# Sums of squares of eight heads: two rounded passes on TensorE in place of one exact one

## The reference, cut to what matters

```python
def group_rmsnorm(o, g):
    B, L, H, dv = o.shape
    of = o.astype(jnp.float32)
    y = of * lax.rsqrt(jnp.mean(of * of, axis=-1, keepdims=True) + EPS)
    y = y.reshape(B, L, H * dv) * g.astype(jnp.float32)
    return y.astype(o.dtype)
```

## Time and profile before

| | |
|---|---|
| median of three runs | 833.07 us |
| the profiled execution's own time | 832.05 us |
| its span | 830.1 us |
| PE busy | 818.5 us, 99% |
| DVE busy | 590.2 us, 71% |
| ACT busy | 374.9 us, 45% |
| POOL busy | 215.6 us, 26% |
| mean granted TensorE clock | 0.992 of full speed |

### The profile page before, as it was taken

One profiled execution on the slowest core, in us unless ns is written; L12 is line 12 of the kernel. 1 busy time (PEld: TensorE's weight loads), 2 busy tenths in 40 slices (PEclk: granted clock), 3 DMA queues, 4 the chain that ended last, 5 costly groups with the idle time before them and its releaser, 6 DMA issues.

```text
span 830.1 us, 15746 instructions
## 1 busy us (share of the span) xinstructions
PE 818.5 (99%) x6544; PEld 807.9 (97%) x6544; DVE 590.2 (71%) x765; ACT 374.9 (45%) x524; POOL 215.6 (26%) x258
## 2 busy tenths in 40 slices
PE   9999999999999999999999999999999999999996
PEld 9999999999999999999999999999999999999996
DVE  5464668477898886767558877777777756878973
ACT  6553234232354553534343644444434424544574
POOL 4018236434335600000430333333223222000020
PEclk9999999999999999999999999999999999999998
DMA  9669967983324984537898497477687863765622
GB/s 273 212 204 164 270 218 164 194 227 134 108 103 93 209 261 140 162 105 263 178 269 229 98 262 223 140 191 186 250 213 203 228 164 96 202 182 168 179 64 107
DMA packets 163025, 152.27 MB, mean 183 GB/s; under 512 B 6677, under 2 KB 144617, under 8 KB 162940
## 3 DMA queue, kind: packets, MB, share of 16 engines
q1 hardware_dynamic: 129420, 109.73, 42.2%
q0 software_dynamic: 33376, 41.04, 26.5%
q10 hardware_dynamic: 160, 0.53, 0.2%
HBM read 145.31 MB, written 58.40 MB: 245 GB/s over the span
## 4 chain that ended last, share of the span: by engine, by line
PE 93%; DVE 4%; issue 1%; DMA 1%; ACT 0%; SPq 0%; DVEq 0%; ACTq 0%
PE mm L2034 51%; PE ax L2327 14%; PE mm L2441 8%; PE ax L2441 6%; PE ax L2053 6%; PE mm L2327 4%; PE ax L2058 2%; PE mm L2114 1%; DVE grs L1453 1%; DMA x_nat<-in_x_prompt 1%; DVE wlo L1443 1%; PE mm L2046 0%; DVE s0g L1623 0%; DVE ylo L1701 0%; DVE wlo L1713 0%
## 5 line engine op out<-in xcount | busy, mean ns | idle before, releaser
L2034 PE MATMUL mm<-nhi,whi 128*128 128x272 f32 x928 | 196.8, 293 | 0.6 <-ACT gqk L1019 0.6
L2034 PE MATMUL mm<-nhi,wlo 128*128 128x272 f32 x928 | 193.4, 290 | 0.0
L2034 PE MATMUL mm<-nlo,whi 128*128 128x272 f32 x928 | 192.7, 289 | 0.0
L1019 ACT ACTIVATE whi<-raw 128x1024 fp32r<-128x1024 f32 (+3 forms) x112 | 128.5, 1181 | 68.8 <-PE mm L2034 38.4
L2034 PEld LDWEIGHTS mm<-nhi,whi 128*128 128x128 f32 x928 | 147.6, 190 | 2.8 <-issue 1.2
L2034 PEld LDWEIGHTS mm<-nlo,whi 128*128 128x128 f32 x928 | 146.9, 190 | 0.0
L2034 PEld LDWEIGHTS mm<-nhi,wlo 128*128 128x128 f32 x928 | 146.4, 191 | 0.0
L1713 DVE TENSOR_TENSOR wlo<-raw,whi 128x1024 fp32r<-128x1024 f32 (+1 forms) x78 | 84.4, 1123 | 5.7 <-ACT whi L1019 3.2
L1443 DVE TENSOR_TENSOR wlo<-raw,whi 128x2048 fp32r<-128x2048 f32 x27 | 64.8, 2398 | 17.5 <-ACT whi L1019 17.4
L950 POOL DMA_DIRECT2D v_sums<-in_w_up x24 | 30.8, 4224 | 117.4 <-DVE mlo L1784 116.8
L1019 ACT ACTIVATE whi<-ring 128x1408 fp32r<-128x1408 f32 x25 | 34.6, 1384 | 44.1 <-PE ax L2441 24.0
(11 more groups left out here) (390 smaller groups left out, 1982.5 us busy)
## 6 DMA issues: line engine op xcount, KB each, us to landing
raw<-in_w_in SPq DMA_DIRECT2D x36, 512.0 KB, 4.9
raw<-in_w_up SPq DMA_DIRECT2D x36, 512.0 KB, 6.9
ring<-w_sums SPq DMA_DIRECT2D x16, 704.0 KB, 4.9
w_sums<-in_w_down SPq DMA_DIRECT2D x9, 768.0 KB, 10.3
w_sums<-in_w_down POOLq DMA_DIRECT2D x9, 768.0 KB, 9.9
ring<-in_w_down SPq DMA_DIRECT2D x9, 704.0 KB, 4.3
v_sums<-in_w_up SPq DMA_DIRECT2D x24, 256.0 KB, 7.1
v_sums<-in_w_up POOLq DMA_DIRECT2D x24, 256.0 KB, 14.4
```

Of the source, the lines that this page charges most:

```text
L1019: return act.activation(out, in_, func, **kw).then_inc(done, 1)
L2034: ins = pe.matmul(mm[:, 2 * j + a, 0:HALF], w, x[:, kx, HALF * a:HALF * (a + 1)], start=first and n == 0 and m == 0, stop=last and n == le ...
```

## The change

The sum of squares over partitions is split as the large products are. ACT squares the head's output twice: once into an fp32r tile (`gsq_high`, a rounded high part), once in float32 into `gsq`. DVE subtracts the high part, in place, which gives `gsq_low`, and counts up a new semaphore `osq_low`. PE waits for that one, and adds four products of 272 columns in fp32r (high and low of each half) instead of two in fp32. A copy of the ones in fp32r type is written once, before the first norm, over the same bytes. The high part has three places: for n below 7 it is one of two by n % 2, of which the even one is the buffer `grs`; so the wait for `o_ready` now stands ahead of the square of norm n and no longer ahead of its root.

```diff
+    gsq_low = at("gsq_low", [P, NT], o_rope, F32R)
+    high_at = [at(f"gsq_high{i}", [P, NT], off, F32R) for i, off in enumerate((o_rope + T, g - T, C + 11 * T))]
+    gsq_high = [high_at[n % 2 if n < 7 else 2] for n in range(2 * HEADS)]
...
+                if n == 0:
+                    st.did(act.activation(ones_r[:, :], ones, ACT.Copy))
+                if n > 1:
+                    act.wait_ge(o_ready, n - 1)
+                st.did(act.activation(gsq_high[n][:, :], normed(NORMS[n]), ACT.Square))
                 run(gsq[:, :], normed(NORMS[n]), ACT.Square, osq_done)
             elif k in ("gn", "rn"):
                 aux_wait_filled(act, s)
-                if norms > 1:
-                    act.wait_ge(o_ready, norms - 1)
                 run(halves(grs2[norms % 2][:, :]), bank2(s), ACT.Sqrt, drained_sem(s), scale=1.0 / DV, bias=eps)
...
+            elif k in ("gsq", "rsq"):
+                n = NORMS.index(("gn" if k == "gsq" else "rn", s[1]))
+                dve.wait_ge(osq_done, n + 1)
+                dve.tensor_tensor(gsq_low[:, :], gsq[:, :], gsq_high[n][:, :].bitcast(F32), ALU.subtract).then_inc(osq_low, 1)
...
+        def summed_parts(name, high, low):
+
+            aux_take(pe, name)
+            for a in range(2):
+                t = HALVES[a]
+                small(bank(name, a)[:, 0:HALF], ones_r[:, :], high[:, t], stop=False)
+                small(bank(name, a)[:, 0:HALF], ones_r[:, :], low[:, t], start=False, done=filled_sem(name) if a else None)
...
             elif k in ("gn", "rn"):
-                pe.wait_ge(osq_done, NORMS.index(s) + 1)
-                summed(s, gsq)
+                pe.wait_ge(osq_low, NORMS.index(s) + 1)
+                summed_parts(s, gsq_high[NORMS.index(s)], gsq_low)
```

More of the change, by code:

```diff
@@ L379, in build @@
     ones = c1[:, C1_ONE:C1_ONE + P]
+    ones_r = at("ones_r", [P, P], a0 + 2 * KD * T + C1_ONE * 4, F32R)
     eps = c1[:, C1_EPS:C1_EPS + 1]
@@ L440, in build @@
     k3_high, k3_ready = sem("k3_high"), sem("k3_ready")
-    osq_done, o_ready = sem("osq_done"), sem("o_ready")
+    osq_done, osq_low, o_ready = sem("osq_done"), sem("osq_low"), sem("o_ready")
     swapped, qk_ready = sem("swapped"), sem("qk_ready")
@@ L2072, in summed @@
             for a in range(2):
-                small(bank(name, a)[:, 0:HALF], ones, sq[:, HALF * a:HALF * (a + 1)],
+                small(bank(name, a)[:, 0:HALF], ones if name == "rstd1" else ones_r[:, :].bitcast(F32), sq[:, HALF * a:HALF * (a + 1)],
                       done=filled_sem(name) if a else None)
+        def summed_parts(name, high, low):
[4 more added lines that the diff above has]
+                small(bank(name, a)[:, 0:HALF], ones_r[:, :], low[:, t], start=False, done=filled_sem(name) if a else None)
         def keep_busy(n):
@@ L2475, in sums @@
             for j in (2 * e, 2 * e + 1):
-                small(mm[:, e, j:j + 1], sq[:, P * j:P * (j + 1)], ones[:, 0:1], start=start and j == 2 * e, stop=stop,
+                small(mm[:, e, j:j + 1], sq[:, P * j:P * (j + 1)], ones_r[:, 0:1].bitcast(F32), start=start and j == 2 * e, stop=stop,
                       done=last_sums if e == 0 and j == 1 else None)
             if e == 1:
-                small(mm[0:NS, e, NJ:NJ + 1], sq[:, SEQ:NT], ones[:, 0:1], start=False, stop=stop,
+                small(mm[0:NS, e, NJ:NJ + 1], sq[:, SEQ:NT], ones_r[:, 0:1].bitcast(F32), start=False, stop=stop,
                       done=last_sums if stop else None)
```

## The result

The changed kernel took 836.26 us (median of 20 runs, 831.45 to 839.84) beside 832.97 us for the kernel before (20 runs, 828.5 to 834.45): a ratio of 1.0047, with a 95% interval of 1.0033 to 1.0062. It is slower: the medians differ by 3.3 us, and the ratio, which comes from all the runs and is not the quotient of the medians, gives 3.9 us. In a later series of 12 runs beside 35 of the kernel before it was 833.61 against 832.74, 1.0028 (1.0008 to 1.0049). The two intervals overlap.

What follows compares the result with a forecast made beforehand. PE, 99% busy, was taken to bound the kernel. Its 3.36 us saved against 7.2 us of new waits, nearly all of DVE's and ACT's making, gave +3.80: 833.07 + 3.80 = 836.9 us, range 834.0 to 839.2.

Steps and rivals of the forecast that it cites:

- rival A: At 220.96 us DVE's second `ysil` product goes ahead of POOL, nothing is held up: D = +1.90, 835.0 us; chance 0.17.
- What bounds: Whole kernel: PE is busy 818.5 of 830.1 us, and a delay it has at 260 us remains at the end.
- What PE saves: At each norm's sums, four fp32r products replace the fp32 ones and save 0.42 us; eight norms save 3.36.
- Norms 1 and 2, the moved wait: Norm 2's square waits for norm 0's multiplication, `wlo` starts late, and PE's transpose at 185.47 is delayed: D = +1.18.
- D: How much later than before, in us, PE is at the same instruction.
- Norm 4's squares: Norm 4's first square waits for norm 2's multiplication, until 209.70; DVE idles 0.70 us and can subtract at 211.03.
- The collision: POOL's masking at 220.96 gets between DVE's two `ysil` products; PE's norm 4 starts at 225.27, not 222.37: D = +2.90.
- the course of the forecast: POOL holds up DVE's second `ysil` product ahead of norm 4, 1.70 us more; 836.9 us at the end; chance 0.50.
- What the collided course costs: Over the eight norms, PE's 3.36 us are saved and 7.2 us of waits appear: D = +3.80.

Runs made afterwards that it cites:

- products alone: Changed kernel with one fp32r square summed twice, no second square or subtraction, `o_ready` wait back at the root; place to place -2.2 us, ratio 0.9978 against before.
- Products later: Changed kernel with a 128x256 MEMSET on DVE ahead of the two `ysil` products; place to place +4.95 us against before, median 838.73 us.
- one product behind: Changed kernel with the second `ysil` product moved from ahead of `s0r` to behind retention head 2's keys; place to place +1.4 us, ratio 1.0011 against before.
- own place for two high parts: Changed kernel with separate room for the high parts of norms 2 and 4, only norm 6 keeping the early wait; place to place +1.0 us, ratio 1.0017.

## Why the prediction was right, and where not

The forecast was 836.9 us (834.0 to 839.2); 836.26 was measured. The direction, the engine and most of the places are right, but the time is met by two courses together: that of rival A, and the forecast one at a higher price.

- **What bounds.** PE's list sets the end and nothing is given back behind 260 us: 569.6 to 569.7 us from there in both. Right.
- **What PE saves.** I took 0.42 us a norm and 3.36 in all. Norms 1, 3, 5 and 6 save that (0.41 to 0.43). But the changed kernel keeps only 0.33 at norm 0, 0.32 and 0.31 at norms 4 and 7, where PE now waits just before (with the products alone it is 0.41 at both), and 0.19 at norm 2: 2.8 us in all, so the term was too large by nearly 0.6. Why the transpose behind norm 2 doesn't follow at once isn't shown.
- **Norms 1 and 2, the moved wait.** D = +1.18 forecast; 184.35 + 2.39 - 185.47 = +1.27 measured. The high part of norm 2 starts at 178.08 (180.47 on the scale of before; 180.35 forecast) and `wlo` at 181.13 (183.52; 183.43 forecast), for 2.29 us (2.28 forecast):

```profile
178.08 0.66 ACT L1160 ACTIVATE gsq_high<-gqk 128x544 fp32r<-128x544 f32 x1 [2.76 <-DVE gqk L1648]
...
179.19 1.90 ACT L1023 ACTIVATE whi<-raw 128x2048 fp32r<-128x2048 f32 x1
```

```profile
179.32 1.52 DVE L1639 TENSOR_TENSOR gsq_low<-gsq,gsq_high 128x544 fp32r<-128x544 f32 x1 [0.72 <-ACT gsq L1023]
181.13 2.29 DVE L1450 TENSOR_TENSOR wlo<-raw,whi 128x2048 fp32r<-128x2048 f32 x1 [0.29 <-ACT whi L1023]
```

  One thing I hadn't foreseen and that cost nothing: POOL's first masking, which lengthened `wlo` before, meets the subtraction instead (1.52 us for 0.72), and that lies in the wait for `whi` anyway.
- **Norm 4's squares.** High part at 207.32 (209.71; 209.75 forecast) behind an idle 3.29 us, the subtraction at 208.56 (210.95; 211.03 forecast). Right within 0.1 us, though for a reason that is not quite the one given: the multiplication of norm 2 took 1.53, still disturbed.
- **The collision: the step that failed.** "Now the two products run from 220.75", and POOL, at 220.96, was to get its turn between them. The products came at 218.26 (220.65), right within 0.1. POOL came at 218.93 (221.32), 0.36 later than forecast, because PE did: 0.09 of that is the longer wait at 185.47, 0.23 what norm 2 failed to save (norm 3 saved its 0.41). So POOL comes about when the second product starts and not 0.2 us behind the start of the first, and the profiled execution goes by rival A: +0.91 at norm 4 (A: 1.00), +0.82 at 243.65 (A: 1.06), 246.03 + 2.39 - 246.97 = +1.45 (A: 1.70), 258.82 + 2.39 - 259.20 = +2.01 at norm 7 (A: 2.32), +1.70 at the end (A: 1.90). Products later shows that the course of the forecast exists with the size given (2.83 for 2.90, 1.64 for 1.70) and the spans speak for its having come in 13 of 20 runs and in 4 of 12. I gave the forecast 0.50 and rival A 0.17; the record calls for about equal chances.
- **What the collided course costs.** Forecast +3.80; measured +4.95, of which up to 1.7 is the half clock behind the wait. Without that about 3.3 would be left. PE's waits there are 7.0 us beside 1.2 before, 5.8 more, where I had 7.2. I had no term for the clock. That the median came out 0.6 us from the forecast is owed to two errors that offset each other: a course that comes only at times, and a price for it that was too small.
- **The Trainium skill's rule** ("SBUF — State Buffer", section "Who interferes with whom") is that a two-input DVE instruction and a GpSimd instruction that reads SBUF exclude each other, and that the earlier one keeps the ports to its end. Rows agree from both sides: POOL 0.03 us behind DVE took 2.44 for 1.90 and DVE nothing more; POOL 0.24 us ahead of where the second product would have started (221.51 + 0.64 - 221.91) left DVE with 1.64 more. With POOL's record 0.04 us ahead (222.98 and 223.02) DVE still went first, so the recorded start is not exactly the moment that decides.

Three parts of the change were priced by runs, added in this order: products -2.2, second square with moved wait +1.3, subtractions +2.6, together +1.7. Alone on the kernel before, the moved wait costs 0.44 and the subtractions 2.0. The second square without the moved wait was not run by itself.

**What stays open.** That the upper group of spans of the changed kernel is the collision is inferred: forcing the race one way puts all 6 spans there, taking the race away puts none of 12 there in each of two kernels (one product behind, own place for two high parts), but no profile of the changed kernel itself fell into it. Why it was 13 of 20 in one series and 4 of 12 in another, and what brings the early half-clock stretches in some executions, wasn't tried.

## What to carry to other kernels

A saving on the engine that is the bound is worth only what the engine that feeds it leaves: here some 3 us saved on products cost eight subtractions on DVE, and eight squares on ACT, in the one stretch where DVE was just in time, and the same change on only those norms whose subtraction fits DVE's idle gaps wins 1.4 us from place to place. Where a forecast turns on which of two engines starts first within a few tenths of a microsecond, it has two outcomes and not one; say the probability of each, look at all the spans of the runs and not only at the profile, and force the race both ways to price it. Compare two profiles from place to place, since spans carry the clock of the one execution.

## What the runs showed of the hardware that wasn't expected

- TensorE's granted clock fell to its half level for a few us near 52 and 151 us, with PE busy (6.00 of 6.00 us), in eight of twelve profiles, at up to 1.7 us each. Of the 81 later executions of the kernel before, the 53 with a mean clock of 0.992 have a mean span of 830.8 us and the 15 with 0.996 one of 828.6, which is more than the 1.7 us of the change.
- A wait of 1.97 us of PE was followed by half clock (0.58 over 4 us), whose cost (up to 1.7 us) was nearly that of the wait; waits of 1.62 us weren't.
- When POOL's masking began between 0.04 us ahead of DVE's second product and 0.12 us behind its start, in three profiles, DVE went first and POOL took 2.34 to 2.50 us for 1.90; with POOL 0.24 us ahead it was DVE that lost 1.64 us, and the stretch took 3.25 us more. One list of instructions thus seems to have two courses.
